# Row buffers of the expert stage: V ring of eight in layer 1 and ten in layer 2, U ring of six and eight

## What is computed

```python
def peer_ffn(h, wq, subkeys, u, v):
    qr = (h @ wq).astype(jnp.float32).reshape(bsz, t, PEER_HEADS, 2, PEER_HALF)
    scores = jnp.einsum('bthpd,hpkd->bthpk', qr, subkeys.astype(jnp.float32))
    s1, i1 = lax.top_k(scores[..., 0, :], PEER_TOPK)
    s2, i2 = lax.top_k(scores[..., 1, :], PEER_TOPK)
    ...
    top, pos = lax.top_k(cand, PEER_TOPK)
    eidx = jnp.take_along_axis(cidx, pos, axis=-1)
    gate = jax.nn.softmax(top, axis=-1).astype(h.dtype)
    ...
    def block(args):
        hk, ek, gk = args
        act = jax.nn.gelu(jnp.einsum('ted,td->te', u[ek], hk), approximate=False)
        return jnp.einsum('te,ted->td', gk * act, v[ek])
```

## Time and profile before

| | us |
|---|---|
| median of 3 runs (4061.87 to 4063.41) | 4062.01 |
| the profiled execution | 4069.16 |
| its span on the core | 4067.4 |
| busy in the span: PE / DVE / POOL / ACT | 3386.7 / 2419.2 / 1588.9 / 1344.5 |

### The profile page before, as it was taken

One profiled execution on the slowest core, in us unless ns is written; L12 is line 12 of the kernel. 1 busy time (PEld: TensorE's weight loads), 2 busy tenths in 40 slices (PEclk: granted clock), 3 DMA queues, 4 the chain that ended last, 5 costly groups with the idle time before them and its releaser, 6 DMA issues. The chain is left out here.

```text
span 4067.4 us, 45097 instructions
## 1 busy us (share of the span) xinstructions
PE 3386.7 (83%) x15340; PEld 2212.7 (54%) x15340; DVE 2419.2 (59%) x5200; ACT 1344.5 (33%) x2779; POOL 1588.9 (39%) x1680
## 2 busy tenths in 40 slices
PE   7989868888888777776867777777699889999899
PEld 3866633333233233322666433332299789999799
DVE  3266555666666667764365666776456465555655
ACT  3255311121112112211364211221244564445543
POOL 0010346666667777775010577777500110000200
PEclk8999989999999999999888899999999999999999
DMA  5222389999999999997222899999745334544244
GB/s 193 96 104 82 111 294 402 416 419 415 419 406 420 405 419 409 419 415 321 79 88 77 323 411 407 419 418 413 312 166 185 114 113 168 186 170 178 76 166 145
DMA packets 246385, 1095.98 MB, mean 269 GB/s; under 512 B 27280, under 2 KB 30608, under 8 KB 227344
## 3 DMA queue, kind: packets, MB, share of 16 engines
q0 software_dynamic: 221184, 805.40, 49.3%
q1 hardware_dynamic: 24976, 287.73, 19.0%
HBM read 1091.97 MB, written 1.05 MB: 269 GB/s over the span
## 5 line engine op out<-in xcount | busy, mean ns | idle before, releaser
L1907 PE MATMUL ps<-v_rows,diagonal 128*128 128x512 f32 x3072 | 1466.4, 626 | 427.8 <-ACT diagonal L1847 400.2
L1787 DVE CUSTOM_DVE_ANT_0 u_rows<-u_rows,ps 128x1024 f32<-128x1024 f32 x768 | 936.2, 1221 | 668.2 <-DMA u_rows<-in_u,experts 655.7
L1907 PEld LDWEIGHTS ps<-v_rows,diagonal 128*128 128x128 f32 x3072 | 581.4, 198 | 1287.8 <-issue 665.2
L1749 POOL DMA_INDIRECT u_rows<-in_u,experts x768 | 732.1, 953 | 354.1 <-issue 210.3
L1759 POOL DMA_INDIRECT v_rows<-in_v,experts x768 | 723.9, 943 | 346.8 <-issue 213.8
L2989 DVE TENSOR_TENSOR weights_low<-ring,weights_high 128x1024 fp32r<-128x1024 f32 (+2 forms) x344 | 396.8, 1162 | 382.0 <-ACT weights_high L2982 380.9
L1838 ACT ACTIVATE hidden<-hidden 128x2 f32<-128x2 f32 x384 | 77.8, 203 | 1616.8 <-DVEq L1789 1616.8
L2620 PE MATMUL ps<-h_high,weights_high 128*128 128x256 f32 x1664 | 486.7, 292 | 17.5 <-DVE h_low L2497 15.2
L2620 PE MATMUL ps<-h_low,weights_high 128*128 128x256 f32 x1664 | 473.7, 285 | 0.0
L2620 PE MATMUL ps<-h_high,weights_low 128*128 128x256 f32 x1664 | 473.4, 284 | 0.0
L2982 ACT ACTIVATE weights_high<-ring 128x1024 fp32r<-128x1024 f32 (+2 forms) x344 | 337.6, 989 | 146.6 <-PE ps L2620 83.1
(11 more groups left out here) (364 smaller groups left out, 4347.1 us busy)
## 6 DMA issues: line engine op xcount, KB each, us to landing
ring<-in_ffn_gu SPq DMA_DIRECT2D x44, 2048.0 KB, 7.9
ring<-in_w_in SPq DMA_DIRECT2D x26, 2048.0 KB, 7.9
ring<-in_w_mod SPq DMA_DIRECT2D x24, 2048.0 KB, 10.1
ring<-in_ffn_down SPq DMA_DIRECT2D x32, 1408.0 KB, 6.0
ring<-in_peer_wq SPq DMA_DIRECT2D x8, 2048.0 KB, 7.9
u_rows<-in_u,experts POOLq DMA_INDIRECT x768, 7.8
v_rows<-in_v,experts POOLq DMA_INDIRECT x768, 7.7
ring<-in_w_out SPq DMA_DIRECT2D x4, 2048.0 KB, 8.0
```

The lines of the kernel that those rows point to most:

```text
L1749: pool.indirect_dma_start(self.UROWS[self.u_slot(n)][:, :], None, m.dram["u"], bass.IndirectOffsetOnAxis(ap=self.IDX[:, n:n + 1], axis=0)) ...
L1787: dve.tensor_tensor_reduce(rows[:, :], rows[:, :], self.rows(), 1.0, 0.0, ALU.mult, ALU.add, self.HID[:, t % 2, s + r:s + r + 1])
L1907: mm = pe.matmul(self.A.ps[:, self.Y_BANK + half, :], self.DIAG[:, (g % DIAGONALS) * GROUP + r, :], rows[:, half * 512:(half + 1) * 512], ...
```

## The change

The three constants become a pair of `Rings`, one for each layer. In layer 1 the V ring has eight buffers (four groups) instead of six, U keeps four in the opening and six behind it. In layer 2 V has ten (five groups), U has eight, all of which are there from the opening on. The number of bytes and of instructions on each engine is the same. `CATCH_UP` keeps the three V groups per U group of the catch-up; the number of V groups that are asked for right at the product's end follows the ring, so it is four instead of three in layer 1. In layer 2 the bound g-1 decides, and it stays three.

```diff
--- before.py
+++ after.py
@@ -1657,18 +1657,26 @@
 GROUP = 2
-U_FIRST = 4
-U_SLOTS = 6
-V_SLOTS = 6
 LAG = 2
 DIAGONALS = 4
-V_AHEAD = V_SLOTS // GROUP
+CATCH_UP = 3
+
+class Rings:
+
+    def __init__(self, u_first, u, v):
+        self.u_first, self.u, self.v = u_first, u, v
+
+ROW_RINGS = (Rings(4, 6, 8), Rings(8, 8, 10))
...
+        self.u_first, self.u_slots, self.v_slots = rings.u_first, rings.u, rings.v
...
     def u_slot(self, n):
-        return n % U_FIRST if n < self.early_rows else (n - self.early_rows) % U_SLOTS
+        return n % self.u_first if n < self.early_rows else (n - self.early_rows) % self.u_slots
...
     def v_until(self, g):
 
-        return min(self.total, max(0, min(g - LAG + 1, V_AHEAD * (g - self.early + 2))))
+        return min(self.total, max(0, min(g - LAG + 1, self.v_slots // GROUP + CATCH_UP * (g - self.early + 1))))
...
     def ask_v(self, pool, v):
         m = self.m
-        if v * GROUP >= V_SLOTS:
-            pool.wait_ge(m.v_weighed.sem, self.at(m.v_weighed, v - V_SLOTS // GROUP + 1))
+        if v * GROUP >= self.v_slots:
+            pool.wait_ge(m.v_weighed.sem, self.at(m.v_weighed, v - self.v_slots // GROUP + 1))
             pool.sem_inc(m.rows_asked.sem, 1)
...
-        UROWS = [m.sb(ctx, f"u_rows_{b}", [P, D]) for b in range(U_FIRST)]
+        rings = ROW_RINGS[layer]
+        UROWS = [m.sb(ctx, f"u_rows_{b}", [P, D]) for b in range(rings.u_first)]
...
-        VROWS = [m.sb(ctx, f"v_rows_{b}", [P, D]) for b in range(V_SLOTS)]
+        VROWS = [m.sb(ctx, f"v_rows_{b}", [P, D]) for b in range(rings.v)]
         Y = m.sb(ctx, "y", [P, D])
         DIAG = m.sb(ctx, "diagonal", [P, DIAGONALS * GROUP, P])
-        UROWS += [m.sb(ctx, f"u_rows_{b}", [P, D]) for b in range(U_FIRST, U_SLOTS)]
+        UROWS += [m.sb(ctx, f"u_rows_{b}", [P, D]) for b in range(rings.u_first, rings.u)]
```

More of the change, by code:

```diff
@@ L1659, with __init__ @@
 GROUP = 2
-U_FIRST = 4
-U_SLOTS = 6
-V_SLOTS = 6
 LAG = 2
 DIAGONALS = 4
-V_AHEAD = V_SLOTS // GROUP
+CATCH_UP = 3
[3 more added lines that the diff above has]
+ROW_RINGS = (Rings(4, 6, 8), Rings(8, 8, 10))
 class Experts:
-    def __init__(self, m, A, n_t, c0, HR, HID, IDX, GATE, keys, UROWS, VROWS, Y, DIAG, plan, last_product, beside=None):
+    def __init__(self, m, A, n_t, c0, HR, HID, IDX, GATE, keys, UROWS, VROWS, Y, DIAG, plan, last_product, rings, beside=None):
+        self.u_first, self.u_slots, self.v_slots = rings.u_first, rings.u, rings.v
         self.m, self.A, self.n_t, self.c0 = m, A, n_t, c0
@@ L1689, in __init__ @@
             m.u_in[self.u_slot(n)].passed(16)
-            m.v_in[n % V_SLOTS].passed(16)
+            m.v_in[n % self.v_slots].passed(16)
     def at(self, sig, n):
@@ L1708, in u_dots_needed @@
         if n < self.early_rows:
-            before = n - U_FIRST
-        elif n - self.early_rows >= U_SLOTS:
-            before = n - U_SLOTS
+            before = n - self.u_first
+        elif n - self.early_rows >= self.u_slots:
+            before = n - self.u_slots
         else:
             slot = self.u_slot(n)
-            before = (self.u_first_uses(slot) - 1) * U_FIRST + slot if slot < U_FIRST else -1
+            before = (self.u_first_uses(slot) - 1) * self.u_first + slot if slot < self.u_first else -1
         return before // GROUP + 1 if before >= 0 else 0
     def v_landed(self, n):
-        slot = n % V_SLOTS
-        return self.m.v_in[slot].sem, self.v_base[slot] + 16 * (n // V_SLOTS + 1)
+        slot = n % self.v_slots
+        return self.m.v_in[slot].sem, self.v_base[slot] + 16 * (n // self.v_slots + 1)
     def v_until(self, g):
-        return min(self.total, max(0, min(g - LAG + 1, V_AHEAD * (g - self.early + 2))))
+        return min(self.total, max(0, min(g - LAG + 1, self.v_slots // GROUP + CATCH_UP * (g - self.early + 1))))
     def place(self, g):
@@ L1758, in ask_v @@
             n = v * GROUP + r
[L1759 to L1760 removed]
+            pool.indirect_dma_start(self.VROWS[n % self.v_slots][:, :], None, m.dram["v"],
+                                    bass.IndirectOffsetOnAxis(ap=self.IDX[:, n:n + 1], axis=0)).then_inc(m.v_in[n % self.v_slots].sem, 16)
     def gpsimd(self, pool):
@@ L1904, in weigh @@
             pe.wait_ge(*self.v_landed(g * GROUP + r))
-            rows = self.VROWS[(g * GROUP + r) % V_SLOTS]
+            rows = self.VROWS[(g * GROUP + r) % self.v_slots]
             for half in range(2):
@@ L2053, in peer @@
             buffers = [m.sb(first, f"weights_{part}", [P, 2, KD * P], F32R) for part in ("high", "low")]
-        VROWS = [m.sb(ctx, f"v_rows_{b}", [P, D]) for b in range(V_SLOTS)]
+        VROWS = [m.sb(ctx, f"v_rows_{b}", [P, D]) for b in range(rings.v)]
         Y = m.sb(ctx, "y", [P, D])
         DIAG = m.sb(ctx, "diagonal", [P, DIAGONALS * GROUP, P])
-        UROWS += [m.sb(ctx, f"u_rows_{b}", [P, D]) for b in range(U_FIRST, U_SLOTS)]
+        UROWS += [m.sb(ctx, f"u_rows_{b}", [P, D]) for b in range(rings.u_first, rings.u)]
         rows = m.sb(ctx, "modulation_rows", [2, 2, 512])
         norm = Norm(m, A, A.x, A.h, norm_streams, split, keep=True)
-        experts = Experts(m, A, n_t, c0, HR, HID, IDX, GATE, keys, UROWS, VROWS, Y, DIAG, plan, m.products + 16)
+        experts = Experts(m, A, n_t, c0, HR, HID, IDX, GATE, keys, UROWS, VROWS, Y, DIAG, plan, m.products + 16, rings)
         opening = Opening(m, A, norm, keys, experts, HR, n_t, c0, plan)
@@ L3205, in program @@
         A.pos = m.sb(early, "pos", [P, T], I32)
-        m.u_in = [Signal(m, f"u_in_{b}") for b in range(U_SLOTS)]
-        m.v_in = [Signal(m, f"v_in_{b}") for b in range(V_SLOTS)]
+        m.u_in = [Signal(m, f"u_in_{b}") for b in range(max(r.u for r in ROW_RINGS))]
+        m.v_in = [Signal(m, f"v_in_{b}") for b in range(max(r.v for r in ROW_RINGS))]
         m.rows_asked = Signal(m, "rows_asked")
```

6 lines of the change are left out of this document (2 added, 4 removed).

## The result

The changed kernel takes 4050.28 us (median of 9 runs, 4048.39 to 4055.66), the kernel before 4063.41 (9 runs, 4058.04 to 4070.75). The ratio is 0.9968, 95% interval 0.996 to 0.9977: 13.1 us faster, between 9 and 16. The forecast was 26 us faster. The time lies in the range, but at the end of it where the rival "only the openings count" put it (4048 to 4052).

A forecast was written before the change was run, and what follows sets the result against it. Transfers at a 420 GB/s ceiling were taken to bound the expert stage, with POOL as tight. Terms of 11 + 7 + 3 + 5 = 26 us off the median of 4062.01 gave 4036, with 4028 to 4052 for 8 in 10.

The forecast's parts named there:

- only the openings count: Rival, chance 0.2: holds vanish mid-stretch but DVE's waits for U rows grow equally; 10 to 14 us remain, 4048 to 4052.
- The bound: Expert stage's gathers: transfers capped at 420 GB/s, 4.99 us a group; POOL as tight, 4.97 to 4.99 us a group.
- unused transfer time: Length x (1 - rate/420) of four stretches: 16.8, 6.2, 8.6 and 13.8 us, 45 in all, the most any request order can win.
- Layer 2, opening: Start of layer 2: early U rows give 0.8 + 1.6 us, the hold before the fourth V group 3.9; 6.3 us together.
- Layer 2, later: Layer 2 behind its opening: three POOL holds on weighed V groups go, 5.3 us; layer taken as 11, bounds 6 and 11.8.
- Layer 1, catch-up: 560:640, V rows catching up: PE's gap and slow clock give 3.9 us, one group's lead 3.5; taken as 7, bounds 2 and 9.
- Layer 1, weight tiles: 640:1290, weight tiles beside gathers: V holds nearly all void as transfers are busy, 6.2 us unused; taken as 3, bounds 0 and 6.
- Layer 1, gathers alone: 1290:1895: three POOL holds of 2.33, 1.83 and 1.92 us all go, less 0.30 each; taken as 5, bounds 3 and 6.6.
- the second rival: The rival "It does nothing that shows": in the tile stretch POOL would be held at dots_done instead of v_weighed; chance 0.11.
- It does nothing that shows: Rival, chance 0.11: U ring or diagonal buffers hold POOL or ACT in place of the V ring; 4055 to 4062.
- Slower: Rival, chance 0.05: at tile bursts more V rows queue ahead of DVE's U row, 2.5 us for each of 13; about 4072.

The follow-up runs named there:

- e3: Kernel before with only layer 2's V ring widened to ten, U left at 4 then 6; requests' lead at row 16 is 4.2 us, no run time given.
- e11: Changed kernel without layer 2's early U buffers (4 then 6) and without the rows_asked increments that nothing waits for; 4048.23 us, ratio 0.9966.
- e4: Kernel before with only layer 2's U ring widened to eight from the opening on, V left at six; layer 2 gains 0.3 us, no run time given.
- e8: Changed kernel with V gathers of 2 KB per row instead of 4, PE weighing the first half twice; 3974.13 us in one run.
- e10: Changed kernel using its larger V rings only from V group 24 of layer 1 and group 8 of layer 2 on; 4062.25 us, ratio 0.9996.
- e9: Changed kernel using its larger V rings only up to V group 24 of layer 1 and group 8 of layer 2; 4052.68 us, ratio 0.9976.
- e5: Changed kernel without the four increments of rows_asked, a signal that nothing waits for; 4047.28 us, ratio 0.9954.
- e12: Changed kernel with a small memset and a drain on POOL ahead of each group's U gathers; 6012.43 us, ratio 1.4798.
- e6: Changed kernel with one more increment of rows_asked behind every U gather; 4048.1 us in one run.

## Why the prediction was wrong

**The bound.** Half right. The transfers' ceiling (421 GB/s at most in any slice) stood, and POOL's pace was a second bound close to it. But the prediction took for lost transfer time what the rate lacks to 420. Where only gathers run, they land every 1.27 us on the mean with either kernel, 4 x 1.27 = 5.08 us for a group and not 4.99: nine longer steps in 480 us stand between those of 1.24. In layer 1 that is the whole of the "unused transfer time" of 8.6 us, and in layer 2 much of the 13.8. It was not open to any ring.

**Layer 2, opening (forecast 6.3).** Right: the requests are 6.0 us ahead at row 16, the dots 6.6 at the end. The share of the early U buffers was too high: with the V ring alone the dots gain 5.3 to 5.8 (e3, e11), so they add some 1 us, not the 0.8 + 1.6, and alone nothing: in e4 the requests are 3.3 us ahead at row 16, but the old V ring's holds are back and by row 240 nothing is left.

**Layer 2, later (forecast 5.3, capped to 11 in sum).** This is a step that failed: "with two more groups of V buffers PE may be that far behind without POOL being held." POOL indeed was not held, and gained the 4 us (requests 6.0 ahead at row 16, 10.0 at row 240; from the product's end to the last gather 12.9 us less, where the forecast said 11). But the dots gained next to nothing of it: the wait for the last part of a gather grew instead (time to landing 7.3 to 8.7 us), and the landings went from one each 1.275 us to one each 1.271. The stage ends with the last landed U row (2896.90 on DVE, 14.0 us before the last copy, and 14.0 in the kernel before), not with POOL's last request. e8 shows how near the other bound is: 668.8 us with a quarter of the bytes gone. The V ring's later use is not worth nothing, though: e10 gains 4.0 us in layer 2 with it, where the larger ring of the opening is missing.

**Layer 1, catch-up (forecast 7, bounds 2 and 9).** The mechanism was right, the size too small: 10.9 us by the dots, 11.6 by the window's bytes, 8.6 in e9, whose catch-up is the same. The first U group was late as told (its dots, at row 28, 2.0 us behind those of the kernel before), and this was made good by row 32. PE's gap went, as told, and with it the half-empty transfers; the window's unused 16.8 us fell to 5.1. The term counted PE's gap and one group of lead, where the unused time of the window had been the better measure.

**Layer 1, weight tiles (forecast 3, bounds 0 and 6).** Within its bounds: the dots' lead rose from 10.9 to 11.7. V holds turned into U holds on `dots_done`, as the second rival said, and at no cost, because the transfers are full: a gather lands each 1.420 us in both kernels. e8 shows that this stretch would get much faster (68 us) with fewer bytes.

**Layer 1, gathers alone (forecast 5, bounds 3 and 6.6).** The step that failed most: "Holds of 2.33, 1.83 and 1.92 us by PE, less 0.30 each, are 5.2 us, and all go." They went, and the lead rose by 0.7 us. The prediction had named the sign of it, GB/s staying at 414 in 1290:1895; it is 414 before and 415 after in 1290:1860. The step was wrong in taking a hold of POOL for a delay of the landings. A gather landed each 1.270 us before and after, and the landings went on at their pace through POOL's holds. The time won on POOL became a longer wait for the last part of each gather, 7.9 to 10.3 us. New holds took the place of the old (2.1, 2.1, 3.4, 1.2 and 2.0 us, once in a hundred gathers), and with these half as long (e5) the dots' lead rose by the same 0.6 us, which fits: neither kind was what bound the stretch. Why a landing comes about 1 us late nine times in this stretch stays open.

**The rivals.** "Only the openings count", given 0.2, is what happened in layer 1, and its time (4048 to 4052) is the measured one. Its sentence "the holds vanish and DVE's waits for U rows grow by the same" is borne out in the gathers alone, where these waits went from 154.3 to 157.8 us. In layer 2 the ring behind the opening counts too (e10). That the time fits is in part luck: the rival gave the openings 10 to 14 us, the table has 10.9 and 6.0 for them, and the medians show less than the profiles. "It does nothing that shows" had the right mechanism for the tile stretch only. "Slower" did not show: no tile cost more.

## What to carry to other kernels

A wait that disappears on the engine that issues transfers counts only if the data then land earlier. Look at three numbers before pricing it. The first is the pace of the landings over a long stretch: if it is the same with and without holds of that engine (1.270 us here), the holds are free. The second is the time from request to landing: if it is well over that of a queue that runs empty (7 to 8 us here, against 4.4 and 5.5 for full-length U rows in e12 and e8), a hold of 2 or 3 us need not delay any landing. The third is the mean pace of the issuing engine, not the pace of undisturbed neighbours. Read the gain from windows that are far under the ceiling: the one at 332 of 420 GB/s gave nearly all of layer 1's, those at 414 to 416 next to nothing, however many holds stood in them.

## What the runs showed of the hardware

- A drain on POOL behind a small memset, with gathers under way, held the next gather until 0.93 us after the last one had landed, 5.2 to 6.5 us in nine of ten cases (e12), and the transfers stood empty in between. Two instructions for a group made the kernel 48% longer.
- Four gathers asked into an empty queue moved 2.12 MB in some 7.5 us (1530.5 to 1538, e12), 280 GB/s; the windows at 410 GB/s and more have 7 us and more from request to landing. The Trainium skill (DMA: Bandwidth & Descriptors, Anatomy of one DMA — SWDGE (gpsimd) path) gives 2.0 us plus the bytes at 436 GB/s, an estimate of 3.2 us for one gather; the shortest V gather of the changed kernel took 4.4, and the median was 10.4.
- A gather is complete with the last of its sixteen parts. In 1300:1780 of the changed kernel fifteen parts were there 7.0 us after the request and the last at 10.3 (medians); in e8, where POOL is the bound, 4.9 and 5.2. So what had lengthened the time to landing there was the wait for one part, not for all.
- With the larger ring POOL stands once in exactly 100 gathers of layer 1, by 1 to 7 us. The place doesn't move with the number of POOL's instructions (e5, e6), so it belongs to the gathers; the length shrinks when requests are held elsewhere (6.9 us in all in e9, 1.4 in e8, where gathers land in 5 us). It is not the larger V ring's alone: e4, with the old one, has three in layer 2 (gathers 1335, 1435 and 1535; 1.3, 1.9 and 4.8 us). What it is stays open. It cost no time that the runs could show.
- Increments of a semaphore between gathers are nearly free on POOL: the median step from one gather to the next is 1.24 us with one more behind each U gather (e6) and with none (e5).
